# A prompt layer in three stages on one core: attention's values as left operands, with another order at the first rows and at both hand-overs

## The reference, cut to what matters

```python
p = rms_norm(x, norm_w) @ w_in                # q, k, v, gate; HGRN's q, f, i, gate
# attention: 128 queries see 16 meta keys, the 128 keys before and their own 128
s = einsum('bnqhgd,bnchd->bnhgqc', q, k) * HEAD_DIM ** -0.5
s = where(mask, s, NEG_BIG)
prob = softmax(concatenate([s, sink_col]), -1)[..., :-1]
o = einsum('bnhgqc,bnchd->bnqhgd', prob, v)
att = o * silu(ga)
hg = rms_norm(hg_o, hg_norm_w) * silu(gh)
y = x + concatenate([att, hg], -1) @ w_out
```

## Time and profile before

| | |
|---|---|
| median of 3 runs | 1170.9 us (1170.76 to 1171.3) |
| the profiled execution's own time | 1167.59 us |
| its span in the profile | 1165.8 us |
| mean granted clock of TensorE | 0.992 of full speed |
| PE busy | 1129.7 us, 97% of the span |
| DVE, ACT, POOL busy | 712.0, 430.4, 362.4 us (61%, 37%, 31%) |

### The profile page before, as it was taken

One profiled execution on the slowest core, in us unless ns is written; L12 is line 12 of the kernel. 1 busy time (PEld: TensorE's weight loads), 2 busy tenths in 40 slices (PEclk: granted clock), 3 DMA queues, 4 the chain that ended last, 5 costly groups with the idle time before them and its releaser, 6 DMA issues.

```text
span 1165.8 us, 26052 instructions
## 1 busy us (share of the span) xinstructions
PE 1129.7 (97%) x9506; PEld 943.5 (81%) x9506; DVE 712.0 (61%) x1847; ACT 430.4 (37%) x1242; POOL 362.4 (31%) x420
## 2 busy tenths in 40 slices
PE   6999999999999999998879999999999999999998
PEld 5877888888888888887667888888888888688887
DVE  6657666666666666668745556555665666655443
ACT  6412212222222222215124555555565665433230
POOL 0003333333333333334422223222322227243331
PEclk9999999999999999999989999999999999999999
DMA  8532111111111111127022511211121133443431
GB/s 281 182 109 74 50 62 63 63 63 63 63 63 54 63 63 63 46 82 270 26 91 74 201 46 45 81 54 45 46 79 59 46 106 133 158 146 144 150 139 72
DMA packets 49391, 108.33 MB, mean 93 GB/s; under 512 B 5088, under 2 KB 17888, under 8 KB 49312
## 3 DMA queue, kind: packets, MB, share of 16 engines
q1 hardware_dynamic: 49328, 107.51, 25.9%
HBM read 70.23 MB, written 38.26 MB: 93 GB/s over the span
## 4 chain that ended last, share of the span: by engine, by line
PE 88%; DVE 5%; POOL 3%; issue 1%; ACT 1%; DMA 1%; SPq 1%; DVEq 0%; POOLq 0%; ACTq 0%
PE h_bank_b L917 5%; PE h_bank_a L917 5%; PE h_bank_b L919 5%; PE h_bank_b L918 5%; PE h_bank_a L919 5%; PE h_bank_a L918 5%; PE o_bank L2621 4%; PE o_bank L2623 4%; PE o_bank L2622 4%; PE h_bank_t L901 3%; PE a_bank_a L1891 3%; PE a_bank_a L1892 3%; PE a_bank_a L1893 3%; PE a_bank_b L1891 3%; PE a_bank_b L1892 3%; PE a_bank_b L1893 3%
## 5 line engine op out<-in xcount | busy, mean ns | idle before, releaser
L917 PE MATMUL h_bank_b<-h_w_hi,h_h_hi 128*128 128x512 f32 x256 | 106.5, 416 | 0.1
L1682 DVE CUSTOM_DVE_ANT_0 a_sm<-a_sc,a_hidden,a_neg_sink 128x272 f32<-128x272 f32 x128 | 59.0, 499 | 74.1 <-PE a_sc L1921 74.0
L917 PE MATMUL h_bank_a<-h_w_hi,h_h_hi 128*128 128x512 f32 x256 | 103.1, 403 | 0.0
L919 PE MATMUL h_bank_b<-h_w_hi,h_h_lo 128*128 128x512 f32 x256 | 100.9, 394 | 0.0
L918 PE MATMUL h_bank_b<-h_w_lo,h_h_hi 128*128 128x512 f32 x256 | 100.4, 392 | 0.0
L919 PE MATMUL h_bank_a<-h_w_hi,h_h_lo 128*128 128x512 f32 x256 | 99.9, 390 | 0.0
L918 PE MATMUL h_bank_a<-h_w_lo,h_h_hi 128*128 128x512 f32 x256 | 99.8, 390 | 0.0
L1488 ACT ACTIVATE a_prb<-a_sm,a_neg_m 128x256 f32<-128x256 f32 x128 | 64.2, 502 | 70.9 <-DVE a_neg_m L1682 70.8
L1891 PE MATMUL a_bank_a<-a_w_hi,a_h_hi 128*128 128x512 f32 (+1 forms) x208 | 77.0, 370 | 6.1 <-DMA a_h_lo<-h_split 6.1
L1892 PE MATMUL a_bank_a<-a_w_lo,a_h_hi 128*128 128x512 f32 (+1 forms) x208 | 74.1, 356 | 0.0
L1893 PE MATMUL a_bank_a<-a_w_hi,a_h_lo 128*128 128x512 f32 (+1 forms) x208 | 74.1, 356 | 0.0
(11 more groups left out here) (327 smaller groups left out, 3121.3 us busy)
## 6 DMA issues: line engine op xcount, KB each, us to landing
h_split<-h_h_hi SPq DMA_DIRECT2D x17, 512.0 KB, 3.0
h_split<-h_h_lo SPq DMA_DIRECT2D x17, 512.0 KB, 3.9
a_h_hi<-h_split SPq DMA_DIRECT2D x17, 512.0 KB, 3.4
a_h_lo<-h_split SPq DMA_DIRECT2D x17, 512.0 KB, 4.3
h_x<-x_prompt SPq DMA_DIRECT2D x16, 512.0 KB, 3.4
o_m<-mixed SPq DMA_DIRECT2D x16, 512.0 KB, 4.0
o_x<-x_prompt SPq DMA_DIRECT2D x16, 512.0 KB, 4.3
y_prompt<-o_x SPq DMA_DIRECT2D x16, 512.0 KB, 2.6
```

The lines of the kernel that those rows point to most:

```text
L917: pe.matmul(out[:, :], h_hi[t.slot][:, k, :], hi, start=(k == 0), stop=False)
L919: ins = pe.matmul(out[:, :], h_lo[t.slot][:, k, :], hi, start=False, stop=(k == KT - 1))
L1682: ins = dve.tensor_tensor_reduce(SM[j % 2][:, i, :], sc[:, i, 0:KEYS], hidden[:, mask, :], -SCALE, neg_sink[:, h:h + 1], ALU.add, ALU.min, ...
```

## The change

**Values.** V's 64 columns of one key-value head become the left operand, and the transposed probabilities of two heads of that key-value head (256 columns) move. The result is the transposed output: head dimension on partitions 0 to 63 for key-value head 0 and 64 to 127 for head 1. A pair of heads is now one from each key-value head (`head(j, kv)`), and `values(t, a)` runs twice a tile, for two pairs at once. The meta part is four matmuls with 128 columns of VMD as left operand. ACT copies the result to MIX (`copy_o`), PE transposes it back to bank_o (`turn_o`, four transposes), DVE's o_norm reads it and writes MIX, and POOL's mix works in place; o_nat is gone. In DVE's order o_norm(last) moves from ahead of place_v to behind maxima 0. On PE `turn_o(last)` stands behind `scores(t0, 0)`, project q is cut in halves of four chunks, and the values stand ahead of turn_p 2 and in the first block of the next tile.

**First rows.** Two weight chunks are split ahead of tile 0's rows.

**First hand-over.** DVE's chunks are cut as 0 and 1; 2 and 3; 4 to 7, the last behind k_norm and place_v. `load_h` of tile 2 stands ahead of the eight spread DMAs and of the waits before them. PE projects six chunks of tile 2 ahead of the sample scores, and its wait for VMD moves behind turn_p(t1, 3).

**Second hand-over.** The sample's high and low rows stand in one left operand (s_rows), two products for each chunk. POOL clears s_rows after the last mix, and makes the low parts of one sum. Splits of sums and the sample's additions move behind other work on DVE. turn_o of tile 15 and of tile 16 have places in the interleaved order.

The diff, cut to its core:

```diff
@@ -459,17 +459,18 @@
-            def split_weights(c):
...
-                for k in range(KT):
+            def split_weights(c, chunks=range(KT)):
...
+                for k in chunks:
                     act.wait_ge(w_loaded[k], 16 * (c + 1))
...
             square_x(tile(0, 0))
+            act.wait_ge(nw_loaded, 16)
+            split_weights(0, range(0, 2))
             split_high(tile(0, 0), 0)
             split_high(tile(0, 0), 1)
-            act.wait_ge(nw_loaded, 16)
-            split_weights(0)
+            split_weights(0, range(2, KT))
             act.wait_ge(lbd, 1)
@@ -1311,13 +1320,14 @@
             sp.dma_start(new_meta_v, v_nat_0[0:META, :]).then_inc(meta_stored, 16)
+            load_h(tile(0, 2))
             yield
...
             for h in range(AH):
-                kv = h // (AH // KVH)
-                sp.dma_start(VMD[h * META:(h + 1) * META, h * HD:(h + 1) * HD], V_meta[:, kv * HD:(kv + 1) * HD]).then_inc(v_meta_spread, 16)
-            load_h(tile(0, 2))
+                kv, g = h // G_HEADS, h % G_HEADS
+                at = g * P + kv * HD
+                sp.dma_start(VMD[h * META:(h + 1) * META, at:at + HD], V_meta[:, kv * HD:(kv + 1) * HD]).then_inc(v_meta_spread, 16)
             yield
@@ -1391,8 +1401,7 @@
                 pool.wait_ge(g_ready, t.n + 1)
-                wait(pool, mix_stored, 16 * t.n)
-                pool.tensor_tensor(MIX[:, :], o_nat[:, :], G[t.slot][:, :], ALU.mult).then_inc(mix_done, 1)
+                pool.tensor_tensor(MIX[:, :], MIX[:, :], G[t.slot][:, :], ALU.mult).then_inc(mix_done, 1)
@@ -1494,10 +1503,17 @@
                 act.wait_ge(p_turned, 4 * (t.n - 1) + j + 1)
-                wait(act, pv_done, 4 * (t.n - 1) + j)
+                wait(act, pv_done, 2 * (t.n - 1) + j // 2)
                 if j == 3:
                     act.activation(PMT[:, :], pt[:, 0, 2 * P:3 * P], ACT.Copy)
-                act.activation(PTS[:, :, :], pt[:, :, 0:2 * P], ACT.Copy).then_inc(p_placed, 1)
+                act.activation(PTS[:, :, :, j % 2, :], pt[:, :, 0:2 * P].rearrange("p a (b q) -> p a b q", b=2),
+                               ACT.Copy).then_inc(p_placed, 1)
...
+            def copy_o(t):
...
+                act.wait_ge(o_ready, 2 * t.n - 1)
+                wait(act, mix_stored, 16 * t.n)
+                act.activation(MIX[:, :], bank_o[:, :], ACT.Copy).then_inc(o_copied, 1)
@@ -1698,16 +1720,17 @@
             def o_norm(t):
-                dve.wait_ge(o_ready, t.n)
+                dve.wait_ge(o_ready, 2 * t.n)
                 dve.wait_ge(rden_done, t.n)
-                wait(dve, mix_done, t.n)
-                dve.tensor_tensor(heads(o_nat[:, :]), heads(bank_o[:, :]), rden[:, :].unsqueeze(2).to_broadcast([P, AH, HD]),
+                by_head = rden[:, :].rearrange("p (x g) -> p x g", x=KVH).unsqueeze(3).to_broadcast([P, KVH, G_HEADS, HD])
+                dve.tensor_tensor(MIX[:, :].rearrange("p (x g d) -> p x g d", x=KVH, d=HD),
+                                  bank_o[:, :].rearrange("p (g x d) -> p x g d", x=KVH, d=HD), by_head,
                                   ALU.mult).then_inc(o_normed, 1)
...
                 dve.wait_ge(v_copied, t.n + 1)
-                wait(dve, pv_done, 4 * (t.n - 1))
+                wait(dve, pv_done, 2 * (t.n - 1))
                 if first_tile(t):
@@ -1721,13 +1744,14 @@
             yield
-            split_weights(1, range(0, 5))
+            split_weights(1, range(0, 2))
             yield
             k_stats(tile(0, 0))
-            split_weights(1, range(5, 8))
+            split_weights(1, range(2, 4))
             dve.wait_ge(knw_loaded, 2 * 16)
...
             place_v(tile(0, 0))
+            split_weights(1, range(4, 8))
             dve.tensor_scalar(neg_sink[:, :], sink[:, :], -1.0, None, ALU.mult).then_inc(sink_negated, 1)
@@ -1804,10 +1828,10 @@
                 gate_plus(t0)
+                place_v(t0)
+                maxima(t0, 0, mask)
                 if tail:
                     o_norm(last)
-                place_v(t0)
-                maxima(t0, 0, mask)
                 if ahead:
@@ -1931,22 +1954,33 @@
-            def values(t, j):
...
-                pe.wait_ge(p_placed, 4 * (t.n - 1) + j + 1)
-                if j == 0:
+            def values(t, a):
...
+                pe.wait_ge(p_placed, 4 * (t.n - 1) + 2 * a + 2)
+                if a == 0:
                     pe.wait_ge(v_placed, t.n + 1)
                     wait(pe, o_normed, t.n)
-                for i in range(2):
-                    h = 2 * j + i
-                    kv = h // (AH // KVH)
-                    c, out = slice(kv * HD, (kv + 1) * HD), bank_o[:, h * HD:(h + 1) * HD]
...
-                    pe.matmul(out, PTS[:, i, 0:P], V[0][:, c], start=(h == 0), stop=False)
-                    ins = pe.matmul(out, PTS[:, i, P:2 * P], V[1][:, c], start=False, stop=False)
+                for block in range(2):
+                    for kv in range(KVH):
+                        c = slice(kv * HD, (kv + 1) * HD)
+                        ins = pe.matmul(bank_o[c, 2 * a * P:2 * (a + 1) * P], V[block][:, c],
+                                        PTS[:, kv, block, :, :].rearrange("p g q -> p (g q)"),
+                                        start=(a == 0 and block == 0), stop=False, skip_group_check=True)
                 ins.then_inc(pv_done, 1)
-                if j == 3:
-                    pe.matmul(bank_o[:, :], PMT[:, :], VMD[:, :], start=False, stop=True).then_inc(o_ready, 1)
+                if a == 1:
+                    for g in range(G_HEADS):
+                        c = slice(g * P, (g + 1) * P)
+                        ins = pe.matmul(bank_o[:, c], VMD[:, c], PMT[:, :], start=False, stop=True, skip_group_check=True)
+                    ins.then_inc(o_ready, 1)
...
+            def turn_o(t):
...
+                pe.wait_ge(o_copied, t.n)
+                for g in range(G_HEADS):
+                    c = slice(g * P, (g + 1) * P)
+                    ins = pe.transpose(bank_o[:, c], MIX[:, c], ident[:, :])
+                ins.then_inc(o_ready, 1)
@@ -1995,14 +2029,14 @@
             pe.wait_ge(h_loaded[0], 64)
-            project(t2, kv_bank(t2), 0, range(0, 4))
+            project(t2, kv_bank(t2), 0, range(0, 6))
             pe.wait_ge(sk_placed, 1)
...
             turn_q(t1, 0)
-            project(t2, kv_bank(t2), 0, range(4, 8)).then_inc(kv_proj, 1)
+            project(t2, kv_bank(t2), 0, range(6, 8)).then_inc(kv_proj, 1)
             pe.wait_ge(q_placed, 1)
@@ -2045,30 +2077,30 @@
                 if tail:
-                    values(last, 3)
+                    values(last, 1)
                 pe.wait_ge(q_placed, 2 * t0.n - 1)
...
                 pe.wait_ge(g_copied, t0.n + 1)
-                project(t1, q_bank(t1), 1, range(0, 5))
+                if tail:
+                    turn_o(last)
+                project(t1, q_bank(t1), 1, range(0, 4))
                 turn_p(t0, 0)
                 scores(t0, 1)
-                project(t1, q_bank(t1), 1, range(5, 8)).then_inc(q_proj, 1)
-                values(t0, 0)
+                project(t1, q_bank(t1), 1, range(4, 8)).then_inc(q_proj, 1)
                 turn_p(t0, 1)
...
                 project(t1, kv_bank(t1), 2, range(0, 4))
-                values(t0, 1)
+                values(t0, 0)
                 turn_p(t0, 2)
...
                 project(t1, kv_bank(t1), 2, range(4, 8)).then_inc(g_proj, 1)
-                values(t0, 2)
                 turn_p(t0, 3)
@@ -2100,38 +2132,38 @@
             project(end, kv_bank(end), 2, range(0, 4))
-            values(t0, 1)
+            values(t0, 0)
             turn_p(t0, 2)
...
             turn_k(end)
-            values(t0, 2)
             turn_p(t0, 3)
...
             yield
-            values(t0, 3)
+            values(t0, 1)
             pe.wait_ge(q_placed, 2 * end.n - 1)
...
             yield
+            turn_o(t0)
             scores(end, 1)
...
             scores(end, 2)
+            turn_p(end, 1)
+            yield
+            scores(end, 3)
             values(end, 0)
-            turn_p(end, 1)
-            yield
-            scores(end, 3)
+            turn_p(end, 2)
+            yield
+            turn_p(end, 3)
+            yield
             values(end, 1)
-            turn_p(end, 2)
-            yield
-            values(end, 2)
-            turn_p(end, 3)
-            yield
-            values(end, 3)
+            yield
+            turn_o(end)
             yield
@@ -2337,6 +2371,8 @@
             yield
+            pool.wait_ge(attention["mix_done"], TILES)
+            pool.memset(s_rows[:, :, :].bitcast(F32), 0.0).then_inc(sums_made, 1)
@@ -2354,6 +2390,10 @@
+            for k in range(HK):
+                pool.wait_ge(w_high, W_DONE + 2 * KT + 2 * HK + k + 1)
+                pool.tensor_tensor(t_lo[0][:, k, :], t_raw[0][:, k, :], t_hi[0][:, k, :].bitcast(F32), ALU.subtract).then_inc(w_ready, 1)
@@ -2505,6 +2546,8 @@
```

(29 more changed lines are left out.)

80 lines of the change are left out of this document (45 added, 35 removed).

## The result

The changed kernel takes 1194.4 us (median of 6 runs, 1191.65 to 1196.93) against 1170.83 for the kernel before. The ratio is 1.0212, with a 95% interval of 1.0198 to 1.0226: 2.1% slower. The forecast was 1174.2, with a range of 1161 to 1187. The sign was right and the size was not; the time lies outside the range.

The account below looks back on a forecast made before the run. TensorE (PE), busy for 97% of the span, was taken as the bound. First rows -1.2, first hand-over -10.0, loop +14.0 and second hand-over +0.5 sum to +3.3, added to the 1170.9 median: 1174.2 us, range 1161 to 1187.

Parts of the forecast that it names:

- The values, PE's work: Attention loop on PE: values, VMD and turn_o fall from 4.27 to 3.63 us, saving 0.64 us a tile.
- Rival (b): Values matmuls: the two column halves don't overlap, +25 us, 1199 us, or 1187 if half overlaps; chance 0.14.
- The values, the waits: Attention loop: new PE waits at turn_p and turn_q, +1.04 and +0.7; period +1.0 us, fourteen tiles +14 (7 to 20).
- First rows: Kernel start: splitting two weight chunks first uses ACT's idle time and starts PE sooner, -1.2 us (0 to -1.7).
- Hand-over 1: Before the attention loop: PE's waits for DVE's chunks and tile 2's h load go, -10 us (-12 to -7).
- Hand-over 2: Attention loop to output stage: later first block, shorter sample product and a stall, sum +0.5 us (-3.3 to +2).
- +1.1: Second hand-over: the first output block's transposes move from 1001.36 to 1002.5, +1.1 us.
- -3.64: Second hand-over: the sample product drops a third of 48 matmuls of 0.23 us on PE, -3.64 us.
- stall of about 3: Second hand-over: PE's fourth block waits about 3 us for add_y behind DVE's last splits and sample additions.
- (c): Attention loop: the clock falls in the new waits, some 2 us a tile, 1200 us; chance 0.04.
- (a): Attention loop: chain slack keeps PE's saving; 1162 us with one wait, 1151 with neither; chance 0.28 for both.
- (d): Hand-overs bring less: the load of h is served no earlier, -3 instead of -10, 1181 us; chance 0.12.

Follow-up runs that it names:

- Experiment 2: The kernel before with one move: in the loop DVE does o_norm of the last tile behind place_v and the first maxima; 1178.9 us, ratio 1.0080.
- 7: The changed kernel with DVE's k_stats of the next tile ahead of o_norm and POOL's k_rstd ahead of mix; 1181.93 us, ratio 1.0112.
- 6: The changed kernel with turn_q(t, 0) on PE moved behind the first twelve matmuls of the next tile's projection; 1180.63 us, ratio 1.0099.
- experiment 1: The changed kernel with one swap in POOL's loop order: k_rstd of the next tile ahead of mix of the last; 1188.18 us, ratio 1.0166.
- experiment 16: The changed kernel with loop and second hand-over reordered, turn_o(15) early, old sample product, and SP's tile 14 store between first rows and W_out; 1157.88 us, ratio 0.9910.
- experiment 12: The kernel before with only the first hand-over's changes; 1164.14 us, ratio 0.9954.
- Experiment 4: The changed kernel with POOL's low parts back on DVE, and last-sum splits and sample additions at their old places on DVE; 1187.01 us, ratio 1.0150.
- experiment 10: The changed kernel with low parts on DVE, one split early, last splits and sample additions at old places, turn_o(16) earlier; 1189.42 us, ratio 1.0170.
- 13: The changed kernel with loop and second hand-over reordered, turn_o(15) early, and the sample's three products and two additions of before; 1161.91 us, ratio 0.9930.

## Why the prediction was right or wrong, point by point

**The values, PE's work: right.** The overlap of the halves was read rightly from the earlier trace rows; a group is 1.01, inside 0.92 to 2.05 and below the 1.14 taken. VMD took 1.00 and not 0.91 (859.21 to 860.21), turn_o 0.44, so the sum is 3.46 against 3.63 forecast and 4.27 before. Rival (b) is out.

**The values, the waits: the mechanism right, the size short.** "+1.0 us a tile" and "Fourteen tiles: +14" came out as 19.0 us (641.39 to 971.06 grew by that much): 13 periods grew by 1.30 on average and tile 15 by 2.16. Both waits are where they were forecast. Experiment 2 makes the wait at turn_p by o_norm's place alone; 7 takes it away and 6 the one at turn_q. POOL's order, which the forecast blamed for the first, is only half of it (experiment 1): DVE's operations beside mix are the other. The turn_p wait, 1.37 from start to start where 0.23 is usual, is 1.14 against 1.20 forecast; that at turn_q 0.62 idle against 0.7. Of the 5 us that were missing, 2.4 are the period (24.77 against 24.6, fourteen times), 1.3 the slower tiles inside the hardware loop (25.03 against 24.77 outside; before, 23.67 against 23.57), whose extra 0.16 a tile no run isolated, and most of the rest SP's load behind the later store, which experiment 16 removes. DVE's operation held by mix (0.17 to 1.17) cost nothing in the changed kernel, since k_rstd stood behind the same mix; it decided experiment 1.

**First rows: wrong, by the clock.** PE did start at 10.94 (forecast 10.75). The gain was 0.26 by 27, and it had become a loss of 1.2 at 65, where the clock was at half for longer than before. This stretch varies between kernels that share the same start (0.50 to 0.86 of full clock over 62 to 66 in the experiments), so the 1.2 is not shown to be the change's.

**Hand-over 1: right in kind, half in size.** "-10": from +1.2 at 65 to -5.8 at tile 1's scores is -7.0, against -8.9 forecast for this part. Tile 1 itself took 1.8 more where I had -1.1: 3.0 were lost at the half clock over 609 to 616, and the remainder, -1.2, is as forecast. The half clock is in experiment 12 too (0.72 over 606 to 618) and not in experiment 1 (1.00), both with this hand-over, so these 3 us are not shown to be the change's either.

**Hand-over 2: this is the step that failed.** "Sum +0.5" came out as +11.4 (26.5 - 15.1). Its terms: the first block, "+1.1", was +2.4; the sample's "-3.64" was right; the "stall of about 3" was 2.3 and 5.7, and the clock behind the first block's wait and the stall took 1.4 and 2.8, a term that the sum had at nothing. The stall was mis-sized because I had costed every DVE operation at its usual duration, four splits at 2.48. That row was itself taken beside POOL's additions, at a moment when POOL was the one that was held. In the changed kernel DVE was: POOL's subtractions and additions lie over DVE's splits and subtractions, which take 6.5 us longer in all. A row to warn of it stood in the trace: from 990.53 six of DVE's splits took 6.96 us beside POOL's sums, 1.16 each. The other part of the stall is the order of work on DVE, with the splits and the sample's additions ahead of add_y. Experiment 4 takes away both and leaves 3.9; no run parts them. The lower bound was added up wrongly too: +1.1 - 3.64 is -2.5 and not -3.3.

This step holds 10.9 of the 23.2 us between the forecast +3.3 and the 26.5 of the profiles. The loop holds 5.0, the first hand-over 4.8 and the first rows 2.4, and of these last two 4.2 came with the half clock.

On this the Trainium skill, "SBUF — State Buffer", section "SBUF: two separate sides", says that GpSimd and a VectorE operation with two SBUF inputs, or one in a two-port mode, share a port pair that one of them holds for its whole instruction while the other blocks. The traces agree in kind. The 128 x 2 operation ends 0.02 us after mix does and the cast of experiment 1 ends 0.15 after it, though no trace tells whether these two, with one input each, ran in such a mode. The subtraction at 1043.05, with one input in PSUM, keeps its 0.68. And the loser can be either engine: DVE in the changed kernel and in experiment 10, POOL in the kernel before and in experiments 4 and 13.

**The rivals.** (c), a clock that falls in the loop's waits, did not happen: the loop kept full clock with waits of 0.98 and 0.62. Half clock did turn up at both hand-overs, where it was not among the rivals. (a) did not. Nor did the cause named in (d), since the load of h came early and PE's wait for it went; but the first hand-over did bring only half.

Still open: what decides whether DVE or POOL is held when they overlap, how the stall of the second hand-over divides between that and the order, and why the tiles inside the hardware loop lose 0.16 more each than before.

## What to carry to other kernels

When a full loop is changed, look at which chains through the other engines were just covered. Here PE's matmuls became 0.8 us a tile shorter, and two idle times of 0.98 and 0.62 opened. Moving a consumer down an engine's queue moves everything behind it and every store and load queued after it: o_norm's later place alone cost 8.6 us with the old values. And do not cost an operation on DVE by one row: look at what POOL did beside it then and will do now, and which of the two was held.

## What the runs showed of the hardware that was not expected

- A DVE operation of 128 x 2 elements took 1.17 us beside a POOL multiplication of 128 x 512 and 0.17 without it; DVE's subtractions of 128 x 512 with both inputs in SBUF took up to 1.8 beside POOL in place of 0.62, and the cast of 128 x 256 took 0.85 in place of 0.29.
- It can also go the other way: one POOL addition of 128 x 512 took 3.86 us (before) and 5.12 us (experiment 4) in place of 1.29, while DVE's subtractions beside it kept 0.62 to 0.68.
- Eight fp32 passes of 256 columns on two column halves take 1.01 us together where the halves' matmuls alternate in the queue, and 1.02 where they come two and two.
- After 0.98 us of idle time in every period of 24.8 the granted clock stayed at full; after 3.2 us it went to half for some microseconds.
